# ConvFFN in a four-layer backbone step: the order of the last iteration's up-projections and outputs

## The reference, cut to what matters

```
h   = modulate(rmsnorm(x, norm2_g), shift2, scale2)
u   = h @ w_in                 # width 1024 -> 2 * 2816
u   = depthwise convolution of width 3 along the tokens, plus bias
g   = silu(first half of u) * second half of u
x   = x + gate2 * (g @ w_out)  # width 2816 -> 1024
```

## Time and profile before

| | |
|---|---|
| time, median of 3 runs | 3312.92 us (3312.91 to 3320.26) |
| the profiled execution's own time | 3312.66 us |
| its span, first to last instruction | 3310.7 us |
| mean granted TensorE clock | 0.963 of full |
| PE busy | 3100.2 us (94%) |
| DVE busy | 2109.5 us (64%) |
| ACT busy | 1069.4 us (32%) |
| POOL busy | 404.0 us (12%) |

### The profile page before, as it was taken

The page is one execution under the profiler, slowest core; times in us unless marked ns, Lnnn a source line. Parts: engine busy times, 40 slices in busy tenths (PEclk is TensorE's granted clock), DMA queues, the critical chain, the costliest instruction groups (busy, mean ns, idle before and its releaser), DMA issues.

```text
span 3310.7 us, 53985 instructions
## 1 busy us (share of the span) xinstructions
PE 3100.2 (94%) x21098; PEld 2820.5 (85%) x21098; DVE 2109.5 (64%) x4290; ACT 1069.4 (32%) x2010; POOL 404.0 (12%) x392
## 2 busy tenths in 40 slices
PE   8999999788889999998989899999989788999998
PEld 6899999765589999997865699999987657999998
DVE  6766666666657666666646566666666664766665
ACT  3322222335533222223335432222222563322221
POOL 3000000223310000003236310000012221000000
PEclk9999999899999999999988999999989799999999
DMA  8433333010033332330200223233321002222111
GB/s 337 191 115 127 114 127 112 23 53 1 1 115 128 115 113 102 114 114 31 77 30 7 90 90 127 90 114 127 115 71 51 4 1 77 77 77 73 66 63 45
DMA packets 47186, 289.93 MB, mean 88 GB/s; under 512 B 4945, under 2 KB 11345, under 8 KB 13265
## 3 DMA queue, kind: packets, MB, share of 16 engines
q1 hardware_dynamic: 47058, 288.21, 23.8%
HBM read 283.98 MB, written 4.21 MB: 87 GB/s over the span
## 4 chain that ended last, share of the span: by engine, by line
PE 87%; DVE 7%; ACT 3%; issue 1%; DMA 1%; POOL 0%; SPq 0%; POOLq 0%; DVEq 0%; ACTq 0%
PE psA L1937 38%; PE psB L1937 25%; PE psA L2038 3%; PE psA L2040 3%; PE psA L2039 3%; PE psB L1953 2%; PE psA L770 2%; PE psB L705 2%; PE psB L687 1%; ACT probs L909 1%; DVE top L1550 1%; PE psB L828 1%; DVE top L1663 1%; ACT pt L857 1%; DMA m_stage<-w_mod_dram 1%
## 5 line engine op out<-in xcount | busy, mean ns | idle before, releaser
L1937 PE MATMUL psA<-h_hi,w_hi 128*128 128x322 f32 (+1 forms) x2848 | 661.8, 314 | 13.7 <-DVE h_lo L2370 13.7
L1937 PE MATMUL psA<-h_lo,w_hi 128*128 128x322 f32 (+1 forms) x2832 | 658.5, 314 | 0.0
L1937 PE MATMUL psA<-h_hi,w_lo 128*128 128x322 f32 x2816 | 649.0, 312 | 0.0
L2397 DVE SCALAR_TENSOR_TENSOR xT<-psB,mod,xT 128x128 f32<-128x128 f32 x1128 | 426.0, 434 | 246.4 <-PE psB L1937 246.4
L1937 PEld LDWEIGHTS psA<-h_hi,w_hi 128*128 128x128 f32 x2848 | 481.7, 191 | 17.0 <-issue 15.7
L1937 PEld LDWEIGHTS psA<-h_lo,w_hi 128*128 128x128 f32 x2832 | 483.2, 191 | 0.0
L1937 PEld LDWEIGHTS psA<-h_hi,w_lo 128*128 128x128 f32 x2816 | 480.7, 191 | 0.0
L2451 DVE TENSOR_SCALAR conv<-u_raw,vec_sb 128x642 f32<-128x642 f32 x176 | 108.3, 616 | 468.7 <-ACT u_raw L2236 468.7
L2282 DVE TENSOR_TENSOR w_lo<-w_stage,w_hi 128x512 fp32r<-128x512 f32 x496 | 346.1, 744 | 29.0 <-ACT w_hi L2155 28.9
L2236 ACT ACTIVATE u_raw<-psA 128x644 f32<-128x644 f32 x176 | 124.6, 708 | 741.5 <-PE psA L1937 741.5
L1937 PE MATMUL psB<-g_hi,wo_hi 128*128 128x322 f32 x1408 | 335.9, 321 | 23.7 <-DVE g_lo L2472 23.7
(11 more groups left out here) (256 smaller groups left out, 4529.4 us busy)
## 6 DMA issues: line engine op xcount, KB each, us to landing
w_stage<-weights_dram SPq DMA_DIRECT2D x124, 1024.0 KB, 4.9
m_stage<-w_mod_dram SPq DMA_DIRECT2D x96, 1024.0 KB, 7.9
wo_stage<-w_out_dram SPq DMA_DIRECT2D x44, 1024.0 KB, 4.8
yT_dram<-xT SPq DMA_DIRECT2D x8, 322.0 KB, 2.2
xT<-xT_dram SPq DMA_DIRECT2D x1, 1544.0 KB, 10.5
xT<-xT_dram SPq DMA_DIRECT2D x1, 1032.0 KB, 7.0
w_stage<-weights_dram SPq DMA_DIRECT2D x2, 512.0 KB, 17.2
rope_raw<-rope_dram SPq DMA_DIRECT2D x3, 256.0 KB, 2.7
```

The source lines that it names most:

```text
L1937: ins = pe.matmul(o, wp, xp[:, a:b], start=first and n == 0, stop=last and n == 2)
L2397: ins = dve.scalar_tensor_tensor(out=xT[:, d, c:c + w], in0=psB[:, bank, at_:at_ + w], scalar=gate[:, d, i:i + 1], in1=xT[:, d, c:c + w], ...
```

## The change

What it does, by engine:

- PE: its loop ends one iteration earlier. After it come, as straight code, u0, u1, u2 and u3 of iteration 10 in a row, then P9, then P10. In P9 the modulation's `mod_half` (ahead of d = 6 and 7) writes psA instead of psB and waits for u3's evacuation. Its transposes (`mod_gap_sum`) stand ahead of d = 3 of P10. In P10, d = 7 waits for the bias.
- New buffers g_hi_last and g_lo_last for iteration 10, in space that the norm leaves free (g_lo_last lies where xs is, which the norm uses).
- ACT: w_out of iteration 10 is rounded in two halves by columns: tiles d = 0 to 3 once P9's d = 3 is done, tiles 4 to 7 once P9 is over. `ghi` of pair 1 is between them, `silu` of pair 1 stands ahead of the last `split_next`.
- DVE: `out_add` of P9 goes into and behind the last convolution, with wo_lo's two halves behind d = 5 and d = 7. The modulation's copies, the last `lo_next` and the bias are put between the adds of P10. Four small memsets clear the edges of the new buffers.
- SP is not edited. What it waits for moves: both halves of `mod_half` (now in P9 behind u3), and the last `lo_next`.

```diff
--- before.py
+++ after.py
@@ -170,6 +170,11 @@
         sq_sum = at("sq_sum", [P, COLS], F32, B_NORM)
         sq = [at(f"sq{i}", [P, COLS], F32, B_NORM + (1 + i) * C) for i in range(2)]
         xs = [at(f"xs{i}", [P, COLS], F32, B_NORM + (3 + i) * C) for i in range(2)]
+
+
+        g_hi_last = at("g_hi_last", [P, 2, COLS], F32R, B_NORM + 5 * C + 4 * (NT + 4) * P)
+        g_lo_last = at("g_lo_last", [P, 2, COLS], F32R, B_NORM + 3 * C)
+        assert B_NORM + 5 * C + 4 * (NT + 4) * P + 8 * COLS <= B_C
 
         mod_rows = at("mod_rows", [P, 4, P], F32, B_NORM + 5 * C + 4 * NT * P)
         assert B_NORM + 5 * C + 4 * (NT + 4) * P <= B_C
@@ -2100,20 +2105,35 @@
                     ins.then_inc(s_wused, 2)
 
                 def out_pass(it, last=False):
+                    gh, gl = (g_hi_last, g_lo_last) if last else (g_hi, g_lo)
+
 
                     pe.wait_ge(s_g[l], it * 2 + 2)
-                    pe.wait_ge(s_wolo, it * 2 + (2 * ITERS * l + 2))
+                    if not last:
+                        pe.wait_ge(s_wolo, it * 2 + (2 * ITERS * l + 2))
                     for d in range(KT):
-                        if d == 0 and l < DEPTH - 1:
+                        if last and d % (KT // 2) == 0:
+                            pe.wait_ge(s_wolo, it * 2 + (2 * ITERS * l + 1 + d // (KT // 2)))
+                        if last and l < DEPTH - 1:
+                            if d == 3:
+                                mod_gap_sum(l, it)
+                            if d == KT - 1:
+                                pe.wait_ge(s_modok, it + (MOD_PASSES * (l + 1) + 1))
+                        if d == 0 and l < DEPTH - 1 and not last:
                             pe.wait_ge(s_modok, it + (MOD_PASSES * (l + 1) + 1))
                         if not (isinstance(it, int) and it == 0 and d < 2):
                             pe.wait_ge(s_oadd[l], it * KT + (d - 1))
                         if d >= KT - 2 and l < DEPTH - 1 and not last:
-                            mod_ffn(l, it + 1, d % 2)
+                            if isinstance(it, int) and it == ITERS - 2:
+                                pe.wait_ge(s_u[l], 4 * ITERS)
+                                mod_half(0, d % 2, it + (6 + MOD_PASSES * l + 2),
+                                         [psA[:, 2 * (d % 2) + c, 3 * P:4 * P] for c in range(2)])
+                            else:
+                                mod_ffn(l, it + 1, d % 2)
                         for f in range(2):
                             ins = product(halves(psB, d % 2),
                                           (wo_hi[:, f, d * P:(d + 1) * P], wo_lo[:, f, d * P:(d + 1) * P]),
-                                          (g_hi[:, f, :], g_lo[:, f, :]), f == 0, f == 1)
+                                          (gh[:, f, :], gl[:, f, :]), f == 0, f == 1)
                         ins.then_inc(s_o[l], 1)
 
                 def ffn_iter(it, first):
@@ -2137,8 +2157,12 @@
 
                 ffn_iter(0, True)
                 ffn_iter(1, False)
-                with pe.Fori(2, ITERS) as it:
+                with pe.Fori(2, ITERS - 1) as it:
                     ffn_iter(it, False)
+
+                for ft in range(4):
+                    u_tile(ITERS - 1, ft, False)
+                out_pass(ITERS - 2)
                 out_pass(ITERS - 1, True)
 
 
@@ -2245,9 +2269,9 @@
                     act.wait_ge(s_conv[l], it * 4 + (2 * p + 1))
                     act.activation(conv[0][:, 1:COLS - 1], conv[0][:, 1:COLS - 1], ACT.Silu).then_inc(s_silu[l], 1)
 
-                def ghi(it, p):
+                def ghi(it, p, dst=g_hi):
                     act.wait_ge(s_gate[l], it * 2 + (p + 1))
-                    act.activation(g_hi[:, p, 1:COLS - 1], conv[1][:, 1:COLS - 1], ACT.Copy).then_inc(s_ghi[l], 1)
+                    act.activation(dst[:, p, 1:COLS - 1], conv[1][:, 1:COLS - 1], ACT.Copy).then_inc(s_ghi[l], 1)
 
                 def ffn_iter(it, first, last):
                     for p in range(2):
@@ -2266,11 +2290,30 @@
                                 act.activation(wo_hi[:, f, :], wo_stage[:, f, :], ACT.Copy).then_inc(s_wohi, 1)
                         ghi(it, p)
 
+                def ffn_last(it):
+                    for ft in range(4):
+                        evac(it, ft, False)
+                        if ft == 3:
+                            silu(it, 1)
+                        if l < DEPTH - 1:
+                            split_next(it, ft)
+                        if ft == 1:
+                            silu(it, 0)
+                            ghi(it, 0, g_hi_last)
+
+                    act.wait_ge(s_wo, it * 16 + 16 * (ITERS * l + 1))
+                    for half in range(2):
+                        act.wait_ge(s_o[l], it * KT - KT // 2 * (1 - half))
+                        c = slice(half * UNIT, (half + 1) * UNIT)
+                        act.activation(wo_hi[:, :, c], wo_stage[:, :, c], ACT.Copy).then_inc(s_wohi, 1)
+                        if half == 0:
+                            ghi(it, 1, g_hi_last)
+
                 ffn_iter(0, True, False)
                 ffn_iter(1, False, False)
                 with act.Fori(2, ITERS - 1) as it:
                     ffn_iter(it, False, False)
-                ffn_iter(ITERS - 1, False, l == DEPTH - 1)
+                ffn_last(ITERS - 1)
 
 
         @block.vector
@@ -2466,11 +2509,11 @@
                     dve.tensor_tensor(conv[1][:, 1:COLS - 1], conv[0][:, 1:COLS - 1], conv[1][:, 1:COLS - 1],
                                       ALU.mult).then_inc(s_gate[l], 1)
 
-                def glo(it, p):
+                def glo(it, p, hi=g_hi, dst=g_lo):
                     dve.wait_ge(s_gate[l], it * 2 + (p + 1))
                     dve.wait_ge(s_ghi[l], it * 2 + (p + 1))
-                    dve.tensor_tensor(g_lo[:, p, 1:COLS - 1], conv[1][:, 1:COLS - 1],
-                                      g_hi[:, p, 1:COLS - 1].bitcast(F32), ALU.subtract).then_inc(s_g[l], 1)
+                    dve.tensor_tensor(dst[:, p, 1:COLS - 1], conv[1][:, 1:COLS - 1],
+                                      hi[:, p, 1:COLS - 1].bitcast(F32), ALU.subtract).then_inc(s_g[l], 1)
 
                 def out_add(it, d):
                     dve.wait_ge(s_o[l], it * KT + (d + 1))
@@ -2527,9 +2570,45 @@
                 assert own.n - own_before == per
                 own.loop = 0
                 own.n = own_before + per * (ITERS - 3)
-                ffn_iter(ITERS - 1, False, l == DEPTH - 1)
-                for d in range(KT):
-                    out_add(ITERS - 1, d)
+
+                def ffn_last(it):
+                    more = l < DEPTH - 1
+                    for b in (g_hi_last, g_lo_last):
+                        own(dve.memset(b[:, :, 0:1].bitcast(mybir.dt.uint32), 0))
+                        own(dve.memset(b[:, :, COLS - 2:COLS].bitcast(mybir.dt.uint32), 0))
+                    for p in range(2):
+                        convolve(it, 2 * p)
+                        if more:
+                            lo_next(it, 2 * p)
+                        convolve(it, 2 * p + 1, (None, 0) if p else (None, None))
+                        if p:
+                            out_add(it - 1, 1)
+                        gate(it, p)
+                        if p:
+                            out_add(it - 1, 2)
+                            out_add(it - 1, 3)
+                        elif more:
+                            lo_next(it, 1)
+                        glo(it, p, g_hi_last, g_lo_last)
+                    for d in range(4, KT):
+                        out_add(it - 1, d)
+                        if d in (5, 7):
+                            half = d // 7
+                            c = slice(half * UNIT, (half + 1) * UNIT)
+                            dve.wait_ge(s_wohi, it * 2 + (2 * ITERS * l + half + 1))
+                            dve.tensor_tensor(wo_lo[:, :, c], wo_stage[:, :, c], wo_hi[:, :, c].bitcast(F32),
+                                              ALU.subtract).then_inc(s_wolo, 1)
+                    for d in range(KT):
+                        out_add(it, d)
+                        if d == 0 and more:
+                            mod_copy_ffn(l, it, 0, psA)
+                            mod_copy_ffn(l, it, 1, psA)
+                        if d == 2 and more:
+                            lo_next(it, 3)
+                        if d == 4 and more:
+                            mod_bias(l + 1, it, mod_parts(psA), it + (MOD_PASSES * (l + 1) + 1))
+
+                ffn_last(ITERS - 1)
```

## The result

| | before | changed |
|---|---|---|
| time, median (range) | 3312.91 us (3310.05 to 3320.26) | 3285.99 us (3285.72 to 3287.27) |
| profiled execution: span | 3310.7 us | 3284.4 us |
| mean granted clock | 0.963 | 0.970 |

The ratio is 0.992 (95% interval 0.9907 to 0.9932): 27 us less, where 30 were forecast. The new time lies within the forecast's range of 3273 to 3296.

A forecast was written before the change was run, and what follows sets the result against it. PE, busy 3100.2 of 3310.7 us, bounds the kernel, so time comes only from its idle stretches or clock. 3312.66 - 23.7 (waits) - 8.5 (slow starts) + 2.0 (new delays) = 3282.5, so 3283 us against the median; range 3273 to 3296.

The forecast's parts named there:

- Removed waits: PE's four waits on g_lo, one at the end of each layer before P10, go: 23.7 us.
- Slow starts of P10: P10's matmuls after each wait, slowed by the clock that fell while PE idled, return to full pace: 8.55 us.
- Rival 2: The clock falls anyway, from the norm's idle time or short stalls; 8.5 us stay lost: 3291, chance 0.06.
- What takes the wait's place: Short PE delays in P9 and P10 for adds and splits: 0.5 us per layer, 2.0 in all.
- DVE has 0.65 to spare each time: In P10, DVE's copies, two w_lo (1.29 us together) and bias fit between adds: 0.65 us spare per 1.79 us tile.
- The delay at tile 6: In P9, tile 6 waits for the add of d = 4, queued behind g_lo on DVE: 0.32 us late.
- Costs put at nothing: Later m_stage and w_in loads, sooner w_in use, the norm, memsets, new buffers and straight code: covered, no term.
- The rest of the program: The clock's other drops, some thirty over the program, shift in phase: sum moves by some 4 us either way.
- The signs it named: No g_lo row, no new psB row over 1 us, P9 and P10 14.3 to 15 us, layers 7 to 8 earlier.
- the three signs of being wrong: P10's first tile waits for wo_lo or an add; later norm over 1 us longer; clock 0.5 in P9 or P10.
- Rival 1: DVE and ACT late in the passes: w_out's second split or g_lo costs 3 us per layer: 3293, chance 0.10.
- Rivals 3, 4 and 5: Loop turns cost: 3274, chance 0.02; the wait stays: 3313, 0.03; psB's double buffering lost: 3366, 0.02.

The follow-up runs named there:

- e6_filler: Kernel before, with 36 unused matmuls put on PE between u3 and the last output pass of each layer: 3309.27 us, ratio 0.9982.
- e3_both: Changed kernel with last two w_lo in P9 behind wo_lo's first half, and g_hi of pair 1 ahead of w_out's first half: 3278.52 us.
- e1_wlo_early: Changed kernel with the last two w_lo in P9, behind wo_lo's first half, instead of behind P10's d = 2: 3281.55 us.
- e4_pool_held: Changed kernel with POOL starting to add the norm's squares only when DVE is done with the last w_lo: 3290.58 us.
- e2_ghi_first: Changed kernel with g_hi of pair 1 ahead of w_out's first half on ACT instead of behind it: 3282.2 us, one run.
- e5_wo_behind: Changed kernel with both halves of w_out rounded only after P9, g_hi ahead of them, wo_lo's halves behind P9's last add: 3306.47 us.

## Why the prediction was right

**Removed waits.** As forecast. The row on g_lo is gone, 23.7 us, and PE goes from u3 to P9 to P10.

**Slow starts of P10, 8.55 us.** As forecast, and now shown: with PE filled during the wait (e6_filler) the clock stays at full and the tails lose 8.1 us, although P10 starts no earlier after g_lo. The 0.4 between the two is P10 at full clock, 14.58 us in the chain and not the 14.47 worked out from an up-projection tile. Rival 2 (the clock falls anyway) is out: P9 and P10 ran at a granted clock of 1 in all four layers.

**What takes the wait's place, 2.0 us.** This term was mis-sized by a factor of four: of the 32.2 us that were to go, the tails lost 24.3 (269.9 to 245.6), so 7.9 took their place, 2.4 in each of layers 0 to 2 and 0.7 in layer 3. The two edits of e3_both give 7.1 of the 7.9 back. Of the last 0.8, 0.4 is the difference of 14.58 and 14.47, and 0.4 I have not traced. The step that failed is the sentence "Against the 1.79 of a tile DVE has 0.65 to spare each time", with the two w_lo at 1.29 from the earlier trace rows. That row was taken beside an idle POOL. In P10, POOL adds squares almost without a break, and each w_lo, which reads two operands from SBUF, ended only after POOL's addition had: 3.46 us for the pair. e1_wlo_early and e4_pool_held show it from both sides, moving the w_lo away from POOL and holding POOL away from the w_lo. By e1_wlo_early it cost 5.7 us. I had counted POOL's own lag in the norm and not what it does to DVE. The Trainium skill ("SBUF — State Buffer", Who interferes with whom) says that DVE and GpSimd share a pair of SBUF ports by an exclusive lock, and that a DVE instruction with two SBUF inputs contends there with a GpSimd instruction that reads SBUF, while one with at most one SBUF input, outside DVE's 2-port modes, does not. The trace agrees in who is held: w_lo (two inputs in SBUF) was, the adds with one input in PSUM were not (1.14 us each).

The rest of that term held roughly. The delay at tile 6, priced at 0.32, was a wait of 0.2 to 0.3, and its cause (g_hi behind w_out's first half) is shown by e2_ghi_first, which takes 0.3 to 0.5 off a tail. Tile 4 had its second half of w_out in time.

**Costs put at nothing.** PE's list has no wait of P9, P10 or the norm behind them for m_stage or w_in, and none in the straight code. The norm kept its place as well: from P10's last matmul to the next mark it took 4.49 us before and after the change. Although the adds bunched behind the w_lo, POOL's last addition in layer 0 ended at 608.01 us and the last square at 607.99, so POOL is now just level with ACT.

**The rest of the program, 4 us either way.** That size was right for the changed kernel (mixers 1.9 less) and too small in general: over ten profiled executions the mixers' sum went from 1152.7 to 1166.2.

**How much of the number is luck.** The tails give 24.3 us, where 30.2 were forecast. The span fell by 26.3, because stages that nobody edited gave the other 2.0: 1.9 in the mixers and 1.0 ahead of the first mark, less 0.9 at the starts of the FFNs. So the mechanism was right, one term was 5.9 us too low, and about a third of that miss was covered by chance.

**The signs it named.** The row on g_lo is gone, the clock is 1 until P10's end, and none of the three signs of being wrong came. Three others failed: PE's list does have a new row at psB with waits over 1 us; P10 took 16.5 us in layers 0 to 2 beside its transposes, and not 14.3 to 15; and the FFNs ended 5.4 to 6.6 us earlier than before each, and not 7 to 8.

**The other rivals.** Rival 1 put the loss at w_out's second split or g_lo, at 3 us per layer. The loss was mostly elsewhere (w_lo, 1.9 us per layer). e5_wo_behind shows that 3 us per layer is about right where w_out is not split: 2.4 there with the clock at full, 3.9 to 4.1 where it fell. Rivals 3, 4 and 5 did not occur.

## What to carry to other kernels

A last iteration whose own chain (evacuate, convolve, gate, split) has nothing to hide behind can borrow the matmuls of the iteration before it, at the price of one more set of operand buffers; price the wait with the slow matmuls behind it, here a third on top (8.1 us on 23.7). When work is moved, look at what the other engines do at its new place, POOL included: here DVE's subtractions with both inputs in SBUF took their usual time only while POOL was not adding, so take such a duration from a row where POOL is as busy as it will be. And compare stretches of the trace between fixed marks, not only totals, since untouched stages can move by more than the edit.

## What the runs showed that I had not expected

- A DVE addition on 8 columns took 1.29 us beside POOL, against 0.17 for it alone (the changed kernel's own row in the next norm is that short). It ended 0.03 us after POOL's addition. So here the hold went by how long POOL's instruction still ran, and not by the DVE instruction's size.
- The hold went both ways. POOL's second addition in P10, which started while the first w_lo was running, took 1.84 us, and the one beside a w_lo in the kernel before 1.83, against 1.57 to 1.60 for the additions behind layer 0 in both kernels that started with no w_lo running.
- A wait of 2.5 us lowered the granted clock in two of four layers (e5_wo_behind), while waits of 1.7 us in the changed kernel did so in none of three. The 5.9 us waits of the kernel before did in all four.
- The mixers of layers 1 to 3, with the same code, took between 1152.7 and 1166.2 us. The stretches of half clock in them begin at other places and last for other lengths from kernel to kernel. The two kernels with the longest mixers also had the lowest clock in them. In the mixer of layer 2 the changed kernel took 440.1 us at a granted clock of 0.93, e5_wo_behind 447.6 at 0.90. That the clock is what moves them fits this, but no run here separates cause from effect.
